# Opening and indexer projection in one program, and layer 0's other modulation and selection moved inside the layer's projection

## The reference, cut to what matters

```
mod = silu(c) @ ada_w[layer] + ada_b[layer]          # (9, 3072) per layer: shift, scale, gate
h = rms_norm(x, norm_g[layer]) * (1 + scale) + shift
qa, ka, va, fa, ga, qb, kb, vb, iq, ik, iw, gb = split_cols(h @ w_in, AB_COLS)
iq, ik = rope(iq), rope(ik)                          # indexer: 8 heads x 64, one key of 64, 8 weights
score = sum over heads of iw * relu(iq . ik)         # per query and key
sel = top_k(score, 256)                              # 132 for sample rows
```

## Time and profile before

| | us |
|---|---|
| median of 3 runs | 1932.09 (1928.14 to 1935.75) |
| profiled execution | 1934.55 |
| its span | 1932.8 |
| TensorE busy | 1689.3 (87%) |
| VectorE busy | 1278.3 (66%) |
| ScalarE busy | 807.9 (42%) |
| GpSimd busy | 224.5 (12%) |

### The profile page before, as it was taken

The page is one execution under the profiler, slowest core; times in us unless marked ns, Lnnn a source line. Parts: engine busy times, 40 slices in busy tenths (PEclk is TensorE's granted clock), DMA queues, the critical chain, the costliest instruction groups (busy, mean ns, idle before and its releaser), DMA issues. The chain is left out here.

```text
span 1932.8 us, 34055 instructions
## 1 busy us (share of the span) xinstructions
PE 1689.3 (87%) x12683; PEld 1321.5 (68%) x12754; DVE 1278.3 (66%) x2813; ACT 807.9 (42%) x1755; POOL 224.5 (12%) x310
## 2 busy tenths in 40 slices
PE   5695679999998985889998998979995999899798
PEld 2463358888876864667776787768784777677687
DVE  2633567887899943678888655561455777777864
ACT  4401452222111203667787224431224776777421
POOL 4101100010000102101110000010004222221000
PEclk8797799999999996899998998989997999999899
DMA  8465612432232319967783643242335111111432
GB/s 296 138 210 187 108 58 71 120 115 93 77 92 67 120 44 218 236 171 218 194 211 141 228 177 126 66 127 85 90 80 110 35 27 45 28 27 51 153 131 98
DMA packets 229996, 235.16 MB, mean 122 GB/s; under 512 B 139797, under 2 KB 164661, under 8 KB 227786
## 3 DMA queue, kind: packets, MB, share of 16 engines
q1 hardware_dynamic: 222954, 213.07, 38.3%
q0 software_dynamic: 6880, 19.92, 2.8%
HBM read 173.98 MB, written 58.95 MB: 121 GB/s over the span
## 5 line engine op out<-in xcount | busy, mean ns | idle before, releaser
L352 PE MATMUL PS<-ab_wh,hT 128*128 128x512 f32 x576 | 231.4, 402 | 4.7 <-DVE ab_wl L688 4.7
L353 PE MATMUL PS<-ab_wl,hT 128*128 128x512 f32 x576 | 226.8, 394 | 0.0
L354 PE MATMUL PS<-ab_wh,hT 128*128 128x512 f32 x576 | 226.2, 393 | 0.0
L1177 DVE TENSOR_SCALAR_CACHE_REDUCE topk_junk<-scores,topk_small 128x528 bf16<-128x528 f32 (+6 forms) x224 | 194.5, 916 | 1.3
L2354 DVE CUSTOM_DVE_ANT_0 la_S<-PS,la_mask 128x128 f32<-128x128 f32 (+3 forms) x144 | 107.6, 747 | 41.7 <-PE PS L354 28.5
L646 ACT ACTIVATE ab_nat<-PS 128x512 f32<-128x512 f32 x54 | 32.3, 597 | 237.1 <-PE PS L354 227.4
L352 PEld LDWEIGHTS PS<-ab_wh,hT 128*128 128x128 f32 x576 | 109.2, 190 | 27.8 <-ACT ab_wh L627 3.9
L354 PEld LDWEIGHTS PS<-ab_wh,hT 128*128 128x128 f32 x576 | 109.2, 190 | 25.3
L353 PEld LDWEIGHTS PS<-ab_wl,hT 128*128 128x128 f32 x576 | 109.1, 189 | 22.1
L352 PE MATMUL PS<-out_wh,out_mT 128*128 128x512 f32 x288 | 116.1, 403 | 4.7 <-DVE out_mT L1830 4.7
L1527 ACT ACTIVATE at_P<-at_S,at_nm 128x128 f32<-128x128 f32 (+2 forms) x144 | 110.5, 767 | 21.3 <-DVE at_nm L1572 21.2
(11 more groups left out here) (413 smaller groups left out, 4301.5 us busy)
## 6 DMA issues: line engine op xcount, KB each, us to landing
ab_wl_raw<-in_ab_w_in SPq DMA_DIRECT2D x64, 256.0 KB, 5.1
out_g<-scratch_gates_nat SPq DMA_DIRECT2D x18, 512.0 KB, 5.5
mod_ada_w<-in_ada_w SPq DMA_DIRECT2D x8, 1024.0 KB, 12.9
mod_w<-in_ada_w SPq DMA_DIRECT2D x16, 512.0 KB, 6.1
mod_w<-in_ada_w SPq DMA_DIRECT2D x8, 1024.0 KB, 6.6
at_kc<-in_cache_a_k SPq DMA_DIRECT2D x8, 1024.0 KB, 8.7
at_vc<-in_cache_a_v SPq DMA_DIRECT2D x8, 1024.0 KB, 8.0
at_kc<-in_cache_b_k SPq DMA_DIRECT2D x8, 1024.0 KB, 8.0
```

The lines of the kernel that those rows point to most:

```text
L352: nc.tensor.matmul(out, x[0], w[0], start=start, stop=False)
L353: nc.tensor.matmul(out, x[0], w[1], start=False, stop=False)
L354: return nc.tensor.matmul(out, x[1], w[0], start=False, stop=stop)
L1177: go(V.tensor_scalar(mark, x, limit, 0.0, op, ALU.add, accum_out=cnt[:, m:m + 1]), 0 if m == M - 1 else 1)
```

## The change

Three edits, none of which changes what is computed.

1. `opening` now holds the indexer projection as well, in one block. One program per engine replaces three. The rows are turned two tiles ahead of the products: TensorE's program is a list of queries' tiles ("q") and narrow tiles ("s"), `IX_ORDER`, and ahead of the products of tile i it turns the rows of tile i + 2. Rows are loaded in five groups (`X_GROUPS`: tile 0, then pairs) through a ring of six; the indexer's weights are loaded right behind the modulation's pieces; the narrow weights come with two DMAs where there were sixteen, and the cached forget logits with four where there were 32. Narrow products are made three tiles at a time, when the last of the three is ready, and the turned tiles of both kinds have their own buffers.
2. `Modulation` leaves the indexer projection and becomes the side work of `projection(nc, c, "ab", ...)`: 32 pieces of 0.5 MB (1024 columns, four matmuls of 256), one behind each of the first 32 steps, in PSUM banks 6 and 7; its bias is added at step 36, transposed at 38 and placed at 40. `index_scores` loses those parts.
3. `selection(nc, c, [4, 4, 5, 5, 2, 2, 5, 5])` gives the passes per step by group: two in the rotary groups, five in the plain ones after the first two.

Core of the diff, the new opening:

```diff
+IX_ORDER = [("q", 0), ("q", 1), ("s", 0), ("q", 2), ("s", 1), ("q", 3), ("s", 2), ("s", 3), ("q", 4), ("s", 4), ("q", 5), ("s", 5),
+            ("q", 6), ("s", 6), ("q", 7), ("s", 7), ("s", 8), ("q", 8)]
+X_GROUPS = [[0], [1, 2], [3, 4], [5, 6], [7, 8]]
+X_RING = 6
+AW = 4
+SMALL = H + DH + H
...
         def _(sp):
             def load_x(i):
-                sp.dma_start(x[:, i, :], x_tile(i)).then_inc(x_in[i // 3], 16)
-
-            def load_w(k):
+                if i >= X_RING:
+                    sp.wait_ge(tr_done, 2 * (i - X_RING) + 2)
+                sp.dma_start(x[:, i % X_RING, :], x_tile(i)).then_inc(x_in[group_of[i]], 16)
...
+            load_ada(0)
+            load_ada(1)
+            load_x(0)
             for k in range(2, KT):
-                load_w(k)
+                load_ada(k)
                 if k == 3:
...
+            for k in range(KT):
+                sp.dma_start(raw[:, k, :], w_ab[k * P:(k + 1) * P, col:col + HD]).then_inc(w_in[k], 16)
+            load_x(1)
+            load_x(2)
+            by_tile = lambda n: c.i[n].rearrange("(i p) d -> p i d", p=P)
+            sp.dma_start(c.ropeC[:], by_tile("rope_cos")).then_inc(rope_in, 16)
+            sp.dma_start(c.ropeS[:], by_tile("rope_sin")).then_inc(rope_in, 16)
+            by_row = w_ab.rearrange("(k p) n -> p k n", p=P)
+            sp.dma_start(sraw[:, :, 0:H], by_row[:, :, 3 * HD:3 * HD + H]).then_inc(small_in, 16)
+            sp.dma_start(sraw[:, :, H:], by_row[:, :, 8 * HD + H:8 * HD + H + DH + H]).then_inc(small_in, 16)
+            sp.dma_start(c.fbias[:], dram(c.i["ab_f_bias"], 0, [[0, P], [1, H]])).then_inc(rope_in, 16)
             for i in range(3, NT):
                 load_x(i)
-            sp.dma_start(c.ropeC[:], c.i["rope_cos"].rearrange("(i p) d -> p i d", p=P)).then_inc(rope_in, 16)
-            sp.dma_start(c.ropeS[:], c.i["rope_sin"].rearrange("(i p) d -> p i d", p=P)).then_inc(rope_in, 16)
-            sp.dma_start(c.ropeCs[:], c.i["rope_cos_short"].rearrange("(i p) d -> p i d", p=P)).then_inc(rope_in, 16)
-            sp.dma_start(c.ropeSs[:], c.i["rope_sin_short"].rearrange("(i p) d -> p i d", p=P)).then_inc(rope_in, 16)
-            sp.dma_start(c.fbias[:], dram(c.i["ab_f_bias"], 0, [[0, P], [1, H]])).then_inc(rope_in, 16)
+            sp.dma_start(c.ropeCs[:], by_tile("rope_cos_short")).then_inc(rope_in, 16)
+            sp.dma_start(c.ropeSs[:], by_tile("rope_sin_short")).then_inc(rope_in, 16)
...
+            for kind, i in IX_ORDER:
+                if kind == "q" and i:
+                    store_q(i - 1)
+                if kind == "s" and i:
+                    store_s(i - 1)
+                if (kind, i) == ("s", 2):
+                    for k in range(PAST // P):
+                        sp.dma_start(c.logf_cache[:, k], c.i["cache_a_logf"][0, :, k * P:(k + 1) * P, :].rearrange("b p h -> p b h")).then_inc(cache_in, 16)
+            store_s(NT - 1)
...
+            squares(0)
+            for k in range(2):
+                split_high(k)
+            act.wait_ge(modT_done, 2)
+            rows_high(0)
+            for k in range(2, KT):
+                split_high(k)
+            squares(1)
+            rows_high(1)
+            act.wait_ge(small_in, 32)
+            nc.scalar.activation(sh[:], sraw[:], ACT.Copy).then_inc(small_hi, 1)
+            for kind, i in IX_ORDER:
+                if kind == "q":
+                    if i in (0, 2, 4):
+                        squares(2 + i // 2)
+                    if i + 2 < NT:
+                        rows_high(i + 2)
+                    if i:
...
             place_modulation(nc, c, 0, 1, PS[:, 7, :], 0).then_inc(modT_done, 1)
             place_modulation(nc, c, 0, 0, PS[:, 7, :], 2).then_inc(modT_done, 1)
+            dve.wait_ge(modT_done, 2)
+            rows_mid(0)
+            for k in range(2):
+                split_low(k)
+            rows_low(0)
+            for k in range(2, KT):
+                split_low(k)
             invert(1)
-            invert(2)
-            dve.wait_ge(modT_done, 2)
+            rows_mid(1)
+            rows_low(1)
+            dve.wait_ge(small_hi, 1)
+            nc.vector.tensor_tensor(sl[:], sraw[:], sh[:], ALU.subtract).then_inc(small_lo, 1)
+            dve.wait_ge(rope_in, 80)
+            turned = {"q": 0, "s": 0}
+            for kind, i in IX_ORDER:
+                if turned["q"]:
+                    dve.wait_ge(q_nat, turned["q"])
+                if turned["s"]:
+                    dve.wait_ge(s_nat, turned["s"])
+                turned[kind] += 1
+                if kind == "q":
+                    if i in (0, 2, 4):
+                        invert(2 + i // 2)
+                    if i + 2 < NT:
+                        rows_mid(i + 2)
+                        rows_low(i + 2)
+                    dve.wait_ge(q_mm, i + 1)
+                    if i >= 2:
+                        dve.wait_ge(q_tr, i - 1)
+                    rope(nc, chain, nat[:, i % 2, :], PS[:, i % 2, :], turn[:], c.ropeC[:, i, :], c.ropeS[:, i, :], H, DH // 2).then_inc(q_nat, 1)
...
+            turn_rows(0)
             pe.wait_ge(biased, 1)
             for b in range(4):
                 last = nc.tensor.transpose(PS[:, 7, b * P:(b + 1) * P], m4[:, b * P:(b + 1) * P], c.ident[:])
             last.then_inc(mod_T, 1)
-            pe.wait_ge(modT_done, 2)
-
-        normed_tiles(nc, c, 0, block, x, scaled, hm, mid, hT)
-
-
-AW = 5
+            turn_rows(1)
+            for kind, i in IX_ORDER:
+                if kind == "q":
+                    if i + 2 < NT:
+                        turn_rows(i + 2)
...
+                        if i == 0:
+                            pe.wait_ge(w_hi, k + 1)
+                            pe.wait_ge(w_lo, k + 1)
+                        last = product(nc, PS[:, i % 2, :], [h[:, k, i * P:(i + 1) * P] for h in hT], [wh[:, k, :], wl[:, k, :]], k == 0, k == KT - 1)
+                    last.then_inc(q_mm, 1)
+                    if i:
...
+                    if i % 3 == 0:
+                        n = i // 3
+                        if n == 0:
+                            pe.wait_ge(small_lo, 1)
+                        else:
+                            pe.wait_ge(across_read, n)
+                        pe.wait_ge(hi_done, i + 3)
+                        pe.wait_ge(lo_done, i + 3)
+                        for k in range(KT):
+                            last = product(nc, PS[0:SMALL, 6, 0:SPAN], [sh[:, k, :], sl[:, k, :]],
+                                           [h[:, k, n * SPAN:(n + 1) * SPAN] for h in hT], k == 0, k == KT - 1)
+                        last.then_inc(across_done, 1)
+                        pe.wait_ge(across_read, n + 1)
```

The side work (`load` first, then `multiply`) and the sharing:

```diff
-        if n >= self.TILES:
+        if n >= self.PIECES:
             return
-        if n >= 3:
-            sp.wait_ge(self.used, n - 2)
-        rows, ada = slice(n // 2 * P, (n // 2 + 1) * P), self.c.i["ada_w"]
-        if n % 2 == 0:
-            sp.dma_start(self.w[:, n % 3, 0:D], ada[0, rows, 2 * D:]).then_inc(self.w_in[n % 3], 16)
...
+        sp.dma_start(self.w[:, n % 2, :], src).then_inc(self.w_in[n % 2], 16)
+
+    def sync(self, sp, s):
+        self.load(sp, s + 2)
...
+    def multiply(self, pe, s):
+        if s < self.PIECES:
+            a, k = s // KT, s % KT
+            pe.wait_ge(self.w_in[s % 2], 16 * (s // 2 + 1))
+            for j in range(4):
+                last = self.nc.tensor.matmul(self.c.PS[32 * j:32 * (j + 1), 6 + a // 2, 256 * (a % 2):256 * (a % 2 + 1)], self.cT[:, k, :],
+                                             self.w[:, s % 2, 256 * j:256 * (j + 1)], start=k == 0, stop=k == KT - 1)
+            last.then_inc(self.used, 1)
...
-def selection(nc, c):
...
     topk = TopK(nc, c, semaphore(nc, "topk_link"), tiles)
+    assert NT * sum(share) >= topk.passes()
     work = []
...
-        for _ in range(-(-topk.passes() // (n - 2)) if s < n - 1 else topk.passes()):
+        for _ in range(share[s // NT] if s < n - 1 else topk.passes()):
...
-                projection(nc, c, "ab", groups, selection(nc, c), weights=weights)
+                side = Modulation(nc, c, cT, inner)
+                projection(nc, c, "ab", groups, selection(nc, c, [4, 4, 5, 5, 2, 2, 5, 5]), side, weights=weights)
```

453 lines of the change are left out of this document (264 added, 189 removed).

## The result

The changed kernel takes 1897.6 us (median of 4 runs, 1897.35 to 1899.63), beside 1933.01 for the kernel before: ratio 0.9827, 95% interval 0.9803 to 0.9851. The forecast was 1901, its range 1887 to 1916. The profiled execution took 1897.83 us, its span is 1896.1. Run again later beside its variants it had 1899.49 us, ratio 0.9833 (0.9805 to 0.9860).

A forecast was written before the change was run, and what follows sets the result against it. The first two stages had idle time; layer 0's projection was bound by TensorE, VectorE as full in its rotary groups. Terms -39 + 0 + 18.2 - 12 = -32.8 from 1934.55 gave 1901.8, forecast as 1901 us, range 1887 to 1916.

The forecast's parts named there:

- Opening and indexer projection, minus 39: Both stages in one program: index scores start at 151.8 us instead of 191.0, bounds minus 58 to minus 17.
- tile 3's wait: Merged opening: 4.0 us ahead of tile 3's transposes, as VectorE waits for all five table loads ahead of its loop.
- Index scores, 0: Index scores: removing the modulation's additions, transposes and placing changes nothing, between minus 2 and plus 2 us.
- Side work, plus 18.2: Layer 0's projection: 32 inserted modulation pieces at 0.55 us plus 0.6 for four transposes; bounds 10 and 34.5 us.
- Rival C: Layer 0's projection: an inserted piece costs 1.06 us however few its columns, 16 us more, 1917; chance 0.05.
- F: Layer 0's projection: each of the 32 pieces arrives late; at 1.5 us a piece the time is 1950; chance 0.02.
- E: Better case: half the opening's 16.1 us of waits overlap and an insertion costs 0.35 us: 1887; chance 0.08.
- Selection, minus 12: Layer 0's rotary groups: two passes a step make TensorE the slower engine, saving 12 us; bounds 0 and minus 12.8.
- D: Layer 0's projection: VectorE didn't stall the rotary groups, or passes return past the last product; 12 us more, 1913; chance 0.06.
- Rival A: Merged opening runs by latency, short waits keeping TensorE at the lower clock for three more products: 1917; chance 0.16.
- Rival G: Merged opening: overlap fails, first product no earlier than before because loads ahead crowd out row tiles: 1924; chance 0.03.
- Rival B: Merged opening: VectorE and GpSimd exclude each other for whole scalings, 22.7 us, of which 10 are slack: 1914; chance 0.05.

The follow-up runs named there:

- part 2 alone: Kernel before with only the other modulation moved from indexer projection and index scores into layer 0's projection, in 32 half pieces: 1926.98 us, ratio 0.9974.
- rows first: Changed kernel with short rotary tables loaded earlier, row tiles 1 and 2 loaded ahead of the last two modulation pieces, and squared and scaled meanwhile: 1898.08 us.
- loads early: Changed kernel with rows first, paired side work and row tiles 3 and 4 loaded right behind the weights: 1890.03 us; with another order at the end too, 1885.14.

## Why the prediction was right, and where its sizes were off

- **Opening and indexer projection, minus 39.** Measured minus 45.0 and minus 41.1. The first product came at 45.95 and 47.0, forecast 48.8. The steps were found where they were put: tile 3's wait (VectorE 3.84 us for the last table, forecast 4.0, of which TensorE shows only 1.3 and, in the second profile, 2.5), 3.6 at the last tile (4.6), 3.8 where two narrow tiles meet (3.4), 1.7 for copies (1.8), 2.7 at the tail (2.3). The prediction took tile 3's wait for one of TensorE's, and there it is too large by some 2 us; the first product was put 2 to 3 us too late, the rest of the stage 0 to 3. In the two other profiles of this opening the stage ends at 149.9 and 149.1, minus 41.1 and 41.9, so minus 39 is closer than the first profile makes it look.
- **What this term is made of** was left open by the prediction, and part 2 alone shows it: some 29 us are the side work's absence, not the overlap of rows and products. The prediction also adds the start to all that follows. The run with rows first has the first product at 37.1 and no earlier end, so up to 9 us of that start are no part of the path that ends the stage, and the same sum would be wrong for that kernel.
- **Index scores, 0.** They took 2.2 and 0.5 us more. Neither is an effect of the change that can be told from chance: the kernels with the program of before had 98.8 and 99.5 us here, the changed kernel's variants 97.5 to 99.5, part 2 alone 100.8. In the changed kernel's first profile, in the 28.5 us behind the first score, the granted clock was lower than before, and the wait list unchanged; before and after:

```profile
201.50:230.00 28.50, 19.74 (x58) 11.37 (x59) 14.04 (x22) 12.56 (x26) 6.87 (x16) 0.68 0.62 102
```

```profile
156.50:185.00 28.50, 19.74 (x48) 10.82 (x49) 12.94 (x22) 11.36 (x22) 6.58 (x16) 0.56 0.60 99
```

  The same 28.5 us hold 48 records of matmuls instead of 58. The eight transposes of the modulation that stood ahead of the scores are gone, but the second profile, without them too, has 57 records, a clock of 0.68 and the stage at 99.3, so their absence alone doesn't explain it; what lowers the clock in one execution and not in the next stays open.
- **Side work, plus 18.2.** Measured plus 23.8. This is the term that was mis-sized: an insertion is 0.74 us and not 0.55, since halving its columns halves only 0.85 of the 1.06 us record, and the step pays some 0.31 whatever columns stand there (0.21 of it inside the record, the rest around it). Rival C (1.06 whatever the columns) was a third of the way right. In the stage TensorE waits once, 3.8 us for the first weights of the block as before, and never for a piece: F falls. So does E, whose insertion of 0.35 is further off.
- **Selection, minus 12.** Measured 12.0, and 12.5 alone. The margin at the end was 8.4 us, forecast 10. D falls.
- **The sum.** Minus 45.0, plus 2.2, plus 11.8, as against minus 39, 0 and plus 6.2: minus 31.0 for the changed stages, forecast minus 32.8. The other 5.7 us of the profiles are nearly all in the branches: 333.6 us before and 322.5 to 331.9 in the profiles of all other kernels, 327.8 in the one that differs from before only in the selection's share. The profile before had a high one, beside 331.9 with part 2 alone. The right total owes part of its closeness to two errors of opposite sign, 6.0 and 5.6 us, and in that it was lucky.
- **Rival A**, products at the lower clock through the whole stage, falls: the mean clock is 0.91 from the first product on, and TensorE's waits there sum to 13.7 us of 100. **Rival G** falls with the first product at 45.9. **Rival B**, the port, was that VectorE and GpSimd wait for each other through a whole scaling of 2.84 us. The nine low halves took 1225 ns in the mean, all alike; before, four of them took 1430 to 1480 beside GpSimd's scaling and the mean was 1318. So the rule of the Trainium skill (SBUF — State Buffer, Who interferes with whom), an exclusive lock on the shared port pair, shows nowhere in them as a wait of a whole scaling. Where the two meet now, GpSimd's instruction is the longer one: 3067 ns in the mean, 2841 before, and 3.5 us in three of nine; that the port does this is consistent with the page and not tested.

## What to carry to other kernels

Price side work that is inserted into a full engine as a fixed part and a part per column (here 0.31 us and 0.43 per 256 columns), and put it in few, large insertions. Ask of a merged stage what each of its edits gives alone: here some 29 of the 41 to 45 us were work moved away from an engine that waited for it, and it cost 24 where it went. A pull at one wait (11.9 us) only moved it to the next tile, because other engines' own rows held the next tile back. Where one engine paces only some of the steps, moving its optional work to the others gives the whole difference, and here it could be read off the spacing of steps beforehand.

## What the runs showed of the hardware

- Four float32 matmuls of 32 output rows each, side by side, cost 0.43 us per 256 columns, and some 0.31 us more for each insertion between wide products; a second piece right behind the first doesn't pay these again (16 insertions fewer, 5.2 us less).
- Profiles of one stage's unchanged program differed where TensorE has pauses, and hardly where it has none: 27 steps took 157.6 us in every profile of the changed kernel and its variants, while the branches took 322.5 to 330.8 with mean granted clocks of 0.92 to 0.94.
- A GpSimd scaling of 128 x 1024 took 2.83 to 2.85 us each of nine times before, and up to 3.52 in the changed kernel, where more of VectorE's work stands beside it. VectorE's subtractions took up to 1.48 us beside it before and kept their 1.22 in the changed kernel; in the two variants with loads early one of them took 1.77 and 1.87.
